# The first expert stage of a three-block model: slabs of rows instead of columns, transposes one pass later, routing by a search

## The reference

```python
def moe_ffn(h, w_router, b_router, w_mlp1, b_mlp1, w_mlp2, b_mlp2):
    T, D = h.shape
    logits = (h @ w_router).astype(jnp.float32) + b_router.astype(jnp.float32)
    top_v, top_i = lax.top_k(logits, TOP_K)
    gates = jax.nn.softmax(top_v, axis=-1)
...
    def expert_block(args):
        xb, e = args
        u = xb @ w_mlp1[e] + b_mlp1[e]
        x_glu = jnp.minimum(u[..., ::2], SWIGLU_LIMIT)
        x_lin = jnp.clip(u[..., 1::2], -SWIGLU_LIMIT, SWIGLU_LIMIT)
        a = x_glu * jax.nn.sigmoid(SWIGLU_ALPHA * x_glu) * (x_lin + 1)
        return a @ w_mlp2[e] + b_mlp2[e]
```

## Time and profile before

| | |
|---|---|
| device time, median of 3 | 2785.68 us (2784.03 to 2789.43) |
| profiled execution: its own time | 2782.02 us |
| its span in the trace | 2780.4 us |
| mean granted TensorE clock | 0.914 of 2.4 GHz |
| busy share of the span | TensorE 85%, weight loads 47%, VectorE 21%, ScalarE 14%, GpSimd 4% |
| DMA over the span | 681.86 MB, mean 245 GB/s |

### The profile page before, as it was taken

The page is one execution under the profiler, slowest core; times in us unless marked ns, Lnnn a source line. Parts: engine busy times, 40 slices in busy tenths (PEclk is TensorE's granted clock), DMA queues, the critical chain, the costliest instruction groups (busy, mean ns, idle before and its releaser), DMA issues.

```text
span 2780.4 us, 31586 instructions
## 1 busy us (share of the span) xinstructions
PE 2359.7 (85%) x12610; PEld 1302.3 (47%) x12611; DVE 577.2 (21%) x1319; ACT 397.0 (14%) x862; POOL 99.2 (4%) x131
## 2 busy tenths in 40 slices
PE   4976598989898889899898988699969899877786
PEld 3855322222222222233234867389966546453343
DVE  1043451111111111111111075300022112130002
ACT  1142111111111111111111144100001112110101
POOL 4000000000000000000000000000000000000000
PEclk9995689999999999999998998799989999978988
DMA  9460569999999699997972475235524334059964
GB/s 291 115 243 0 193 248 367 387 373 386 374 386 383 250 382 378 386 372 294 371 293 98 151 262 194 75 137 159 152 99 144 114 114 144 31 227 377 404 261 195
DMA packets 302121, 681.86 MB, mean 245 GB/s; under 512 B 15922, under 2 KB 57139, under 8 KB 289504
## 3 DMA queue, kind: packets, MB, share of 16 engines
q1 hardware_dynamic: 264176, 535.79, 53.2%
q0 software_dynamic: 37856, 144.98, 14.4%
q10 hardware_dynamic: 16, 0.02, 0.0%
HBM read 679.70 MB, written 1.06 MB: 245 GB/s over the span
## 4 chain that ended last, share of the span: by engine, by line
PE 69%; DMA 17%; DVE 7%; SPq 3%; ACT 3%; issue 1%; DVEq 0%; ACTq 0%
PE ps L667 29%; PE ps L969 15%; DMA ring<-in_w_mlp 11%; PE ps L991 5%; DMA MOD<-in_w 5%; PE ps L1262 3%; PE ps L973 2%; PE ps L732 2%; SPq L455 2%; PE ps L941 2%; PE ps L1000 2%; PE ps L834 1%; DMA ring<-in_w_ada 1%; PE ps L742 1%; DVE stat L1721 1%
## 5 line engine op out<-in xcount | busy, mean ns | idle before, releaser
L969 PE MATMUL ps<-ring,scr 128*64 128x512 f32 x1680 | 528.6, 638 | 98.5 <-DMA ring<-in_w_mlp 96.8
L969 PEld LDWEIGHTS ps<-ring,scr 128*64 128x64 f32 x1680 | 159.5, 147 | 416.2 <-issue 415.3
L667 PE MATMUL ps<-ring,HTY 128*128 128x512 f32 (+5 forms) x960 | 326.3, 501 | 3.7 <-ACT HTY L1343 3.7
L667 PE MATMUL ps<-HTY,ring 128*128 128x256 f32 (+2 forms) x1392 | 298.8, 385 | 2.4 <-ACT HTY L1343 2.4
L667 PEld LDWEIGHTS ps<-HTY,ring 128*128 128x128 f32 (+2 forms) x1392 | 248.0, 182 | 51.3 <-ACT HTY L1343 3.7
L969 PE MATMUL ps<-MOD,scr 128*64 128x512 f32 x560 | 247.8, 595 | 0.0
L991 PE MATMUL ps<-HTY,scr 128*64 128x512 f32 x560 | 246.1, 592 | 1.0 <-ACT scr L1509 1.0
L991 PE MATMUL ps<-scr 128*64 128x512 f32 x560 | 246.1, 592 | 0.0
L667 PEld LDWEIGHTS ps<-ring,HTY 128*128 128x128 f32 x960 | 174.7, 190 | 152.0 <-issue 136.0
L2116 DVE TENSOR_SCALAR scr<-ps 128x256 f32<-128x256 f32 x70 | 29.7, 424 | 867.9 <-PE ps L973 867.8
L991 PEld LDWEIGHTS ps<-HTY,scr 128*64 128x64 f32 x560 | 76.6, 137 | 159.9 <-issue 159.9
(11 more groups left out here) (416 smaller groups left out, 2169.5 us busy)
## 6 DMA issues: line engine op xcount, KB each, us to landing
ring<-in_w_mlp SPq DMA_DIRECT2D x96, 2048.0 KB
MOD<-in_w_mlp SPq DMA_DIRECT2D x32, 2048.0 KB
HTY<-in_w_mlp POOLq DMA_DIRECT2D x32, 2048.0 KB, 10.2
scr<-in_w_mlp POOLq DMA_DIRECT2D x32, 2048.0 KB, 16.3
ring<-in_w_ada SPq DMA_DIRECT2D x24, 2048.0 KB, 9.5
ring<-in_w SPq DMA_DIRECT2D x48, 1024.0 KB, 10.5
ring<-in_w_in SPq DMA_DIRECT2D x21, 2048.0 KB, 7.8
ring<-in_w_ff SPq DMA_DIRECT2D x16, 2048.0 KB, 8.9
```

Of the source, the lines that this page charges most:

```text
L667: mm = pe.matmul(o, lhs(k), rhs(k), start=begin and k == 0, stop=end and k == nk - 1)
L969: pe.matmul(ps[C1 * s:C1 * (s + 1), b, :], XG[:, k, :], m1_slabs[2 * b + s][:, k, :], start=k == 0, stop=False)
```

## The change

- **Slabs of rows.** Slab j of `w_mlp1` is now 256 rows with all 2048 columns, two consecutive rows to a partition: a run of 16 KB. Slab 4 or 5 of `w_mlp2` is 512 rows, as two groups of 256 with two rows to a partition: runs of 8 KB. An up product goes through slabs 0 to 3 in turn and adds to four groups of columns in two banks, and the four bias products stand at the end. The whole bias row comes in one DMA.
- **Given back one by one.** Slabs 0, 1 and 2 have a semaphore each (`m1_slab_used`), slab 3 goes by the end of the up product (`m1["up"]`). GpSimd still asks for slabs 4 and 5 after the down product.
- **Order on TensorE.** Both halves' transposes move into the next pass: `up(n,0)`, `turn_hidden(n-1,0)`, `gather(n+1)`, `turn_hidden(n-1,1)`, `turn_tokens(n+1)`, `down(n-1)`, `up(n,1)`, `scatter(n-1)`, `back(n)`. The two turns use the same bank in turn, so the second waits for ScalarE's copy of the first. The down product waits for slab 5 only in its second half.
- **One activation.** VectorE and ScalarE work on both halves at once, after the end of the up product.
- **Routing.** The 8 greatest logits are found by `max` and marked by `match_replace` (four values of 1e30 stand in front, so that four real ones remain); the mask alone releases the rank products. The gates' transposes and the first sums move behind the up product of pass 0 (`start_sums`). VectorE makes only the list of experts and an offset for each pass; it picks places and gates by a register from `EPLACE` and `GT`. The table `c_before` goes.
- **First slabs.** GpSimd asks for slab 5 of expert 0 once the mixer's output is ready, and for slab 4 as before.

```diff
-END1 = OF_PASS + PASSES
+END1 = OF_PASS + PASSES + 2
...
-        m1_slabs = [shaped(ring[:, j, :], (KT, BANK)) for j in range(3)] + [
-            MOD[:, 1:5, :].rearrange("p m (h n) -> p (m h) n", h=2), shaped(HTY[:, :], (KT, BANK)), carve(9216, KT, BANK)]
...
+        m1_slabs = [shaped(ring[:, j, :], (2, 2 * F1)) for j in range(3)] + [
+            MOD[:, 1:5, :].rearrange("p (k m) d -> p k (m d)", k=2), shaped(HTY[:, :], (4, D)), carve(9216, 4, D)]
...
             def expert_slab(e, j):
-                cols_ = slice(BANK * j, BANK * (j + 1))
-                sp.dma_start(b1row[32 * j:32 * j + 1, :], I["b_mlp1"][0][e:e + 1, cols_] if isinstance(e, int)
-                             else I["b_mlp1"][0][bass.ds(e, 1), cols_]).then_inc(m1_landed[j], 16)
-                sp.dma_start(m1_slabs[j], kpn(I["w_mlp1"][0][e][:, cols_])).then_inc(m1_landed[j], 16)
+                sp.dma_start(m1_slabs[j], I["w_mlp1"][0][e][2 * P * j:2 * P * (j + 1), :].rearrange("(p k) n -> p k n", p=P)).then_inc(m1_landed[j], 16)
+            def expert_row(e):
+                sp.dma_start(b1row[0:P:32, :], I["b_mlp1"][0][bass.ds(e, 1), :].rearrange("e (c n) -> (e c) n", c=4))\
+                    .then_inc(m1_row_landed, 16)
...
+            expert_row(0)
             sp.wait_ge(m1["counted"], 1)
             with sp.Fori(1, E1) as e:
                 through = sp.value_load(work[0:1, bass.ds(e + (THROUGH - 1), 1)], min_val=1, max_val=PASSES)
-                for j in range(4):
-                    sp.wait_ge(m1_up[j // 2], through)
+                for j in range(3):
+                    sp.wait_ge(m1_slab_used[j], through)
                     expert_slab(e, j)
+                sp.wait_ge(m1["up"], through)
+                expert_slab(e, 3)
+                expert_row(e)
             n_passes = sp.value_load(work[0:1, 0:1], min_val=E1, max_val=PASSES)
-            sp.wait_ge(m1_up[1], n_passes)
+            sp.wait_ge(m1["up"], n_passes)
...
+            def expert_slab(e, j):
+                pool.dma_start(m1_slabs[j].rearrange("p (t k) n -> p t k n", t=2),
+                               I["w_mlp2"][0][e][BANK * (j - 4):BANK * (j - 3), :].rearrange("(t p k) n -> p t k n", t=2, p=P))\
+                    .then_inc(m1_landed[j], 16)
+            pool.wait_ge(mix_ready, 1)
+            expert_slab(0, 5)
             pool.wait_ge(h2_ready, NT)
...
             vector(4)
             vector(5)
...
             expert_slab(0, 4)
-            pool.wait_ge(gates_ready, 1)
-            expert_slab(0, 5)
...
-            pe.wait_ge(gates_ready, 1)
...
-            pe.wait_ge(moe1_params_landed, 32)
...
+            pe.wait_ge(m1["masked"], 1)
...
-            pe.wait_ge(product_free, end["gates1T"])
...
+            def start_sums():
+                pe.wait_ge(gates_ready, 1)
+                for a in range(NT):
+                    mm = pe.transpose(ps[0:E1, 7, P * a:P * (a + 1)], GT[:, a, :], ident[:, :])
+                mm.then_inc(m1["gates_turned"], 1)
+                pe.wait_ge(m1["gates_read"], 1)
+                pe.wait_ge(moe1_params_landed, 16)
+                for a in range(NT):
+                    for half in range(2):
+                        pe.matmul(sum_bank(a, half), gatesT[:, P * a:P * (a + 1)], b2row[:, BANK * half:BANK * (half + 1)],
+                                  start=True, stop=False, skip_group_check=True)
...
-                for k in range(4):
-                    mm = pe.transpose(ps[:, 3, P * k:P * (k + 1)], XS[:, P * k:P * (k + 1)], ident[:, :])
+                for jj in range(2):
+                    for i in range(2):
+                        k = 2 * jj + i
+                        mm = pe.transpose(ps[:, 3, P * k:P * (k + 1)], XS[:, S * jj + i:S * (jj + 1):2], ident[:, :])
...
             def up(n, b, e):
+                if b == 0 and not (isinstance(n, int) and n == 0):
+                    pe.wait_ge(m1["up_read"], n)
                 for j in (2 * b, 2 * b + 1):
-                    pe.wait_ge(m1_landed[j], 32 * e + 32)
-                if not (isinstance(n, int) and n == 0):
...
+                    if j == 3:
+                        pe.wait_ge(m1_row_landed, 16 * e + 16)
+                    pe.wait_ge(m1_landed[j], 16 * e + 16)
+                    for i in range(2):
+                        for c in range(4):
+                            mm = pe.matmul(ps[C1 * (c % 2):C1 * (c % 2 + 1), c // 2, :], XG[:, 2 * j + i, :],
+                                           m1_slabs[j][:, i, BANK * c:BANK * (c + 1)], start=j + i == 0, stop=False)
+                    if j < 3:
+                        mm.then_inc(m1_slab_used[j], 1)
+                if b == 1:
+                    for c in range(4):
+                        mm = pe.matmul(ps[C1 * (c % 2):C1 * (c % 2 + 1), c // 2, :], ones[32 * c:32 * c + 1, 0:C1],
+                                       b1row[32 * c:32 * c + 1, :], start=False, stop=True)
+                    mm.then_inc(m1["up"], 1)
...
             def turn_hidden(n, b):
...
+                pe.wait_ge(m1["hidden"], n + 1)
+                if b == 0:
+                    pe.wait_ge(m1["back_read"], n + 1)
+                else:
+                    pe.wait_ge(m1_turn_read[0], n + 1)
+                for i in range(2):
+                    mm = pe.transpose(ps[:, 2, P * i:P * (i + 1)], aS[:, b, i:S:2], ident[:, :])
+                mm.then_inc(m1_turn[b], 1)
             def down(n, e):
-                pe.wait_ge(m1["turn_read"], 2 * n + 2)
-                pe.wait_ge(m1["back_read"], n + 1)
+                pe.wait_ge(m1_turn_read[1], n + 1)
...
-                                       m1_slabs[4 + s][:, k, :], start=k == 0, stop=k == KT - 1)
+                    for t in range(2):
+                        for i in range(2):
+                            for s in range(2):
+                                mm = pe.matmul(ps[C1 * s:C1 * (s + 1), 2, :], aT[:, 2 * (j - 4) + i, C1 * t:C1 * (t + 1)],
+                                               m1_slabs[j][:, 2 * t + i, BANK * s:BANK * (s + 1)],
+                                               start=j + t + i == 4, stop=j + t + i == 7)
...
-                if e_before is not None:
-                    turn_hidden(n - 1, 1)
-                    gather(n + 1)
-                    down(n - 1, e_before)
-                    turn_tokens(n + 1)
-                    up(n, 1, e)
-                    scatter(n - 1)
-                else:
-                    up(n, 1, e)
-                    gather(n + 1)
-                    turn_tokens(n + 1)
-                turn_hidden(n, 0)
+                turn_hidden(n - 1, 0)
+                gather(n + 1)
+                turn_hidden(n - 1, 1)
+                turn_tokens(n + 1)
+                down(n - 1, e_before)
+                up(n, 1, e)
+                scatter(n - 1)
                 back(n)
...
-            expert_pass(0, 0, None)
+            pe.wait_ge(m1["gather_read"], 1)
+            up(0, 0, 0)
+            up(0, 1, 0)
+            start_sums()
+            gather(1)
+            turn_tokens(1)
+            back(0)
...
-            def ranks(dst, v, groups, n, c1, c2, order):
...
-            dve.wait_ge(moe1_params_landed, 32)
...
+            step(dve.memset(LOGITS1[:, :, 0:4], 1.0e30))
             dve.wait_ge(product_free, end["route1"])
...
+            step(dve.tensor_tensor(LOGITS1[:, :, 4:], LOGITS1[:, :, 4:], both(b_router), ALU.add))
             for a in range(NT):
-                ranks(GT[:, a, :], LG[:, a, :], 1, E1, cmp1, cmp2, before)
...
-            tell(dve.tensor_scalar(MASK[:, :, :], GT[:, :, :], float(TOP1), None, ALU.is_lt), route_shift, 1)
+                step(dve.max(TOPL[:, a, :], LOGITS1[:, a, :]))
+                step(dve.match_replace(CHOSEN1[:, a, :], TOPL[:, a, :], LOGITS1[:, a, :], -1.0e30))
+            tell(dve.tensor_tensor(MASK[:, :, :], CHOSEN1[:, :, 4:], LOGITS1[:, :, 4:], ALU.not_equal), m1["masked"], 1)
+            tell(dve.tensor_tensor(LX[:, :, :], LOGITS1[:, :, 4:], TOPL[:, :, 4:5].to_broadcast([P, NT, E1]), ALU.subtract), route_shift, 1)
...
+            def picked(n):
+                shape = [P, NT, C1]
+                tell(dve.tensor_tensor(PICK[:, :, :], both(iota[:, 0:C1]), rcur.unsqueeze(2).to_broadcast(shape), ALU.is_equal),
+                     m1["pick"], n + 1)
+            def pick(e, offset, n, astep):
+                astep(dve.tensor_copy(gcur.unsqueeze(2), GT[:, :, bass.ds(e, 1)]))
+                astep(dve.tensor_scalar(rcur.unsqueeze(2), EPLACE[:, :, bass.ds(e, 1)], offset, None, ALU.subtract))
+                picked(n)
+            def pick_back(n):
+                shape = [P, NT, 2, C1]
+                tell(dve.tensor_tensor(PICKG[:, :, :, :], PICK.unsqueeze(2).to_broadcast(shape),
+                                       gcur.unsqueeze(2).unsqueeze(3).to_broadcast(shape), ALU.mult), m1["pick_back"], n + 1)
...
+            step(dve.scalar_tensor_tensor(EPLACE, place, far, MASK[:, :, :], ALU.add, ALU.mult))
```

(36 more changed lines are left out.)

199 lines of the change are left out of this document (56 added, 143 removed).

## The result

The changed kernel takes 2705.5 us (median of 4; 2691.8 to 2709.6) against 2785.7: a ratio of 0.970, interval 0.968 to 0.972, 80 us faster. The direction was forecast and the range holds the time, but the forecast gain was 27 us: a third of it. The profiled execution has a span of 2699.8 us, 80.6 less than before.

The account below looks back on a forecast made before the run. The prediction took the first expert stage as bound by DMA, with TensorE 4 us per pass behind. Loop -12, start -18 and end +3 summed to -27 us: 2755 for the profiled execution, 2759 for the median, range 2660 to 2850.

Parts of the forecast that it names:

- the rate: Expert slabs' DMA: longer runs raise it from 386 to 424 GB/s, a slab taking 4.95 us instead of 5.43.
- the right case: Expert stage's queues: bytes go 2 : 1 for SP against GpSimd, 2755 to 2759 us, chance 0.50.
- TensorE's pass without waits: One unstalled expert pass on TensorE after the change: 28.46 us, bounds 27.6 and 29.2.
- wait in down: TensorE waits for slab 5 in the down product: 3.7 us a pass.
- lower clock behind it: TensorE's slower clock after the wait in the down product: 0.6 us added per pass.
- loop: Expert passes between the issues of the second matrix's slabs: 1019 us against 1031.7, -12 us.
- start: Start of the expert stage: shorter ranking, first up product at 337.4, loop at 365.5, -18 us.
- end: End of the expert stage: both turns behind the last scatter, hidden chain uncovered, +3 us (bounds 0 and 5).
- SP's first byte at 4.6: SP's queue delivers its first data 4.6 us after down ends, leaving GpSimd's queue 2.0 us alone.
- Packet by packet: DMA engines alternate between queues by packets, so the longer packets of SP's queue get bytes 2 : 1.
- Even shares: Rival: queues share bytes evenly, slabs land at 20.8 us, nothing waits, 2673 us; chance 0.24.
- the slower one: Rival: GpSimd's packets stay 4 KB against SP's 16 KB, bytes 4 : 1, landing at 32.8, 2861 us; chance 0.14.

Follow-up runs that it names:

- the repeated run: The changed kernel once more, with no edit, timed again: 2706.8 us, ratio 0.971.
- the late first slab 5: Changed kernel, but slab 5 of expert 0 is asked for after slab 4, as before the change: 2709.1 us, ratio 0.971.
- the slow ranking: Changed kernel with ten instructions of 1024 elements put back on VectorE ahead of the search: 2720.0 us, ratio 0.975.
- the unhindered loop: Changed kernel with slab 5 fetched only for expert 0 and its old content used afterwards: 2663.8 us, ratio 0.956.
- all three repairs: Changed kernel with the first matrix in 8 KB runs, with slab 4 asked for early, or with both: 2678.2, 2682.2 and 2679.0 us.

## Why the prediction was wrong in size

The direction, the bound, the rate, the shares and the place of the new wait were right. The greatest chance stood on the right case; its size was wrong. Term by term, as the prediction put them, each against the profiled execution:

| term | forecast | measured | difference, us |
|---|---|---|---|
| TensorE's pass without waits | 28.46 | 27.96 | 32 passes: -16 |
| wait in down | 3.7 in 25 passes, 92 in all | 48.1 in all, 1.7 a pass | -44 |
| lower clock behind it | 0.6 in 25 passes, 15 | 957.8 - 32 x 27.96 - 48.1 = 15 | 0 |
| loop | -12 | -73.9 | -62 |
| start | -18 | -7.3 | +11 |
| end | +3 | +0.6 | -2 |

The "measured" column is one execution. In three other profiled ones with the same loop (the repeated run, the late first slab 5, the slow ranking) the waits are 45 to 46 us and what is left beside them and the 894.4 us of the unhindered loop is 20 to 26 us instead of 15. So the agreement in the term of the clock is luck: it was forecast for waits twice as long.

- **The step that failed** is "SP's first byte at 4.6 (slab 2 used up at 3.45, signal and issue 1.1)". The issue did come at 3.8, the first byte only at 7.2: in the pass at 456.35 GpSimd's queue was alone for 4.6 us instead of 2.0. By the prediction's own sum the landing then comes at 7.2 + 3 x (9.9 - 4.6) + 0.4 = 23.5, before it is needed. But a queue that starts isn't at full rate at once: until SP's first packet GpSimd's had moved 1.72 of its 4.19 MB, which at 424 GB/s is 4.1 us' worth. With that the sum is 7.2 + 3 x (9.9 - 4.1) + 0.4 = 25.0, and measured are 25.4. In the pass at 425.69 SP's queue still had bytes of the last request until 2.4 us behind GpSimd's issue; GpSimd's had moved 1.54 MB by SP's first packet, which gives 26.5 against 27.2 measured. Against the need at 24.7 the waits are 0.8 and 2.5 us, not 3.7. That the time alone is what decides is shown by the kernels that change it and little else: longer by asking in pairs (-17 us), longer by asking early (-23), none at all by a late request (+283).
- **TensorE's pass** was mis-sized by the bias products: four side by side take as long as two, the lower bound that the prediction named and did not take. The turns that now wait for ScalarE cost 0.26 and not 0.3 to 0.4.
- **Packet by packet** was right; the sizes of the rivals on the shares were not. Even shares were given 2673 and measured 2678 once the runs were made equal, but the slabs land 25.3 us behind the down product there and not at 20.8, so the time was met by luck; the slower one was given 32.8 and 2861, and measured 34.2 and 2950. By the Trainium skill's rule ("DMA: Bandwidth & Descriptors", queues, rings and completion order) an engine goes round robin at packet granularity. Taken for what the profile counts as a packet, the three pairs of sizes here (16 with 8, 8 with 8, 16 with 4 KB) all agree, with packets equal within 3%.
- **How near the kernel was to "slower"** was summed wrongly: from a pass of 32.8 us to 33.9 it is 1.1 us, and at three for one a first byte of GpSimd's 0.4 us later is enough, not 0.9.
- **The rate** was right: 427 GB/s with both queues, 386 once the runs were 2 KB again. It is the greater part of the gain: without it 17 us are left. The same page of the Trainium skill, specifications, sets 512 B as the size for line rate. Here runs of 2 KB fell 9 to 10% short of 8 and 16 KB.
- **The start** was right up to the first up product and wrong behind it. Four rows of the timeline after, as in the earlier trace rows:

```profile
323.40 7.03 PE L667 MATMUL ps<-wr,HTY 128*128 128x32 f32 x32 [0.69 <-ACT HTY L1357]
...
342.44 13.44 PE L973 MATMUL ps<-ring,scr 128*64 128x512 f32 x48 [0.69 <-ACT scr L1509]
...
362.13 7.19 PE L930 MATMUL ps<-scr 32*128 32x512 f32 x8 [1.49 <-ACT scr L1543]
...
376.34 8.42 PE L973 MATMUL ps<-ring,scr 128*64 128x512 f32 x32 [2.02 <-issue]
```

The router's product begins 4.2 us later than before (319.21 there), in code that the change doesn't touch. The window from 144 to 162 us shows why:

```profile
144.00:162.00 18.00, 13.37 (x166) 8.95 (x164) 9.69 (x23) 9.39 (x21) 0.00 (x0) 0.72 0.26 86
```

The granted clock of this stretch of the mixer is 0.72, where it was 1.00 before and in the repeated run. It is below 1 in nine of the thirteen traces of the changed kernel and its variants and 1.00 in four, so the start differs from execution to execution: in the repeated run, without this dip, the loop begins 11.7 us earlier than before. Whether the change makes the dip more frequent isn't shown, with one trace of the kernel before. Less these 4.2 the first up product is 18.7 us earlier, against 19.5 forecast. But between the up product and the loop lie 16.1 us and not 9.5: the sums take 7.19 us at the low clock of this stretch, as they did before, and 9.0 with the gates' transposes and their read, where the prediction had 4.5. The row with the 7.19 was among those it rested on. The rest up to the loop takes 7.1 and not 5.0.
- **The end** costs less than the 3 forecast: uncovered behind the last `back` are three waits of 0.8, 0.6 and 0.6 us, and from the last issue of slab 4 to the last scatter it is 48.1 us instead of 47.7. The +0.6 of the whole stretch can't be told from noise: in the other kernels with the same code behind the loop it takes 1343 to 1358 us.

## What to carry to other kernels

When two queues feed one set of DMA engines, write down the packet size of each before changing a layout: the bytes are shared as the packets are long, and the queue whose data the compute engine will wait for should not be the one with the shorter packets. Making both 8 KB was worth 27 us here, asking for slab 4 3.5 us earlier 23, and a request 2.8 us later, which also let the other queue start first, cost 10 us of a later landing. Release a buffer early only where the early request doesn't take bandwidth from one that is more urgent. And once the engines are full in every pass, count the bytes: all three repairs end at the same 928 to 932 us.
